# Blocks of 64 tokens of two head pairs in place of chunks of 128 tokens of one pair in a chunked RWKV-7 scan

## The chip, the cores and the metric

The kernel runs on one core of one Trainium2 chip. The metric is the device time of one execution, from the first to the last instruction on the slowest (here the only) core, in microseconds (us). It is written for the engines directly: each engine has its own list of instructions, in the order in which the program writes them, and semaphores are the only link between engines.

## What is computed

One layer of a bidirectional RWKV-7 model on 1024 latent and 128 context tokens, width 1024, 16 heads of 64. Only the scan matters here. For each head and direction it runs over the tokens:

```
def step(S, inp):
    r_t, w_t, k_t, v_t, a_t, b_t = inp
    sa = jnp.einsum('bhvk,bhk->bhv', S, a_t)
    S = S * w_t[:, :, None, :] + sa[..., None] * b_t[:, :, None, :] + v_t[..., None] * k_t[:, :, None, :]
    return S, jnp.einsum('bhvk,bhk->bhv', S, r_t)
```

The latent scans start from a given state, the context scans from zero; the context's final states are outputs. The forward and backward results are added, normalised per head (`lnx`), scaled, given a bonus term and a gate. Ahead of the scan stand the projections of all operands, behind it the output projections and the MLP.

## The kernel before, in words

Three stages follow each other. The **projection stage** goes over the 8 pairs of heads (a pair fills the 128 partitions). It projects the operands of a pair with TensorE, VectorE (DVE) makes the decays' running sums (`decay_sums`) and the operand planes (`operands`), and SyncE (SP) stores these in DRAM: `op_d`, `v_d`, and in `x_d` the inverses of the 16x16 diagonal blocks, which DVE makes by `substitution`. The **scan stage** takes them back. The **product stage** is the three 1024x1024 products and the MLP, by a seven-product scheme on quadrants.

The scan stage turns the recurrence into small matrix products over a chunk of `C = 128` tokens. Its unit is one chunk of one pair in both directions (forward chunk j and backward chunk 7-j together): `UNITS` = 8 pairs x 9 chunks = 72. The chunk's triangular system is inverted by doubling: 16 to 32 to 64 to 128 tokens, one level a round, `LATE = LEVELS - FIRST = 3` levels. Round `s` of the loop (one per engine, `for s in range(-4, UNITS)`) holds, on TensorE (PE) in this order:

- `turn(s)`: transposes of the partial inverses `xt` of the three units in flight; `token_major(s+1)`: four 128x128 transposes of the operands of the next unit; `ur_state(s)`: state times operands;
- `gram(s+4, d)` for the two directions, the products between tokens of the unit four ahead, in pieces 0, 1 (128 moving columns) and 2 (256 columns); DVE masks each into `gmat` (DVE's `gram`, L2126, 128x1024 elements);
- `serial_ur`, `serial_u`, `serial_s`, `serial_y`, `y_state`: the serial part of unit `s`. ACT copies `ur` (L1656) and `up` (L1660) out of PSUM between them; DVE's `states` makes the state of the next unit (L2180, one fused instruction per direction), which `ur_state(s+1)` waits for;
- `left(s)` and `right(s)`: one inverse level for each of the three units in flight. `left` needs `tc` (DVE `turned`, L2132), `xtb` (POOL `trimmed`) and `lm` (POOL `start_inverse`); ACT copies its result (`product_out`, L1643, tile `p`) for `right`; DVE's `summed` (L2143) adds it to `xt` for the next round. The last level's result goes through ACT (`last_blocks`) and POOL (`triangles`, L900) into `tt`, which `serial_u` reads;
- the finals of one 128-token chunk of one pair, from round 5 on: `variance`, ACT's square root (L1690), DVE's `reciprocal` (L2209), `spread` and `gate` on PE, then DVE's `scaled` (L2214, L2218, L2221), and SP stores `xa_d`. After the last unit five finals are left over (`TAIL`);
- in two rounds of each nine a piece of the modulation (`modulation`, `modulation_turned`).

In the rows of the page and the trace the PE lines are those of helpers (L972 is `mm`), so a step is told by its tiles: `inv<-ident,xt` is `turn`, `bank<-ident,ub` `token_major`, `ser<-state,ub` `ur_state`, `gbank<-ub` `gram`, `ser<-vb,gmat` `serial_ur`, `bank<-ident,fstd` `spread`, `inv<-xtb,...` `left`, `ser<-ub,state` `y_state`, `ser<-ur,tt` `serial_u`, `inv<-p,tc` `right`, `ser<-...,tok` `serial_s`, `ser<-gmat,...` `serial_y`, `bank<-gl,pl` `gate`, `bank<-bones,fsq` `variance`. Operands named `64*64` use a quarter of the array (one of two row halves and one of two column halves), `128*64` half of it. Each f32 product shows as two matmul records, a transpose as one.

## Time and profile before

| | |
|---|---|
| median of 3 runs | 2689.25 us (2687.86 to 2693.72) |
| span of the profiled execution | 2688.9 us, with 67501 instructions |
| PE busy | 2568.6 us, 96% |
| DVE busy | 1872.8 us, 70% |
| ACT busy | 1081.2 us, 40% |
| POOL busy | 1188.7 us, 44% |
| chain that ended last | PE 85%, DVE 8%, issue, ACT and DMA 2% each |

The profile gives no other time of the profiled execution than its span; the span is 0.35 us under the median of the runs. PE's busy time counts a matmul from its start to its modelled end, so neighbours overlap and a gap shorter than about 0.2 us (the length of the shortest matmul record) does not show. The difference between the starts of two steps is what a step costs. The granted clock of PE is 1.00 nearly throughout, and 0.5 where it is at half speed.

### The profile page before, as it was taken

Reading aid. Unit: us, or ns where it says so; the run is one execution under the profiler, and the core shown is the slowest. Engines: PE = TensorE matmul, PEld = TensorE weight load, DVE = VectorE, ACT = ScalarE, POOL = GpSimd, SP = SyncE. Lnnn points to the kernel's source line nnn. Section 1 sums busy time; section 2 is a strip of 40 time slices with the busy share of each in tenths; the row PEclk is TensorE's granted clock in tenths of the full one; section 3 lists DMA queues with packets and bytes.
Section 4 is the critical chain, followed back from the end, with each engine's and each line's share of the span. In section 5 each row is a group of like instructions: output and inputs, shape, how many; then the busy total and the mean of one; then the engine's idle time right before and its main releaser. Section 6 shows DMA issues by size and latency. Waiting matters only on the chain.

```text
span 2688.9 us, 67501 instructions
## 1 busy us (share of the span) xinstructions
PE 2568.6 (96%) x28608; PEld 2413.9 (90%) x28608; DVE 1872.8 (70%) x2978; ACT 1081.2 (40%) x1978; POOL 1188.7 (44%) x1154
## 2 busy tenths in 40 slices
PE   4899999999999998999999998999799999999998
PEld 3899999999999996777777777999799999999998
DVE  3365675856758565787666657799778678677686
ACT  3434243342433422433333333443453453443534
POOL 1323232322323225555555545656446556565662
PEclk8999999999999999999999998999899999999999
DMA  8333425334254364445454456453223332333231
GB/s 325 106 102 118 140 71 186 113 111 140 80 175 123 101 203 116 131 133 149 142 155 139 145 162 181 133 179 98 61 63 86 81 101 63 87 82 100 63 79 71
DMA packets 282409, 329.10 MB, mean 122 GB/s; under 512 B 76288, under 2 KB 215936, under 8 KB 273536
## 3 DMA queue, kind: packets, MB, share of 16 engines
q1 hardware_dynamic: 274448, 278.66, 33.4%
q0 software_dynamic: 5904, 39.32, 6.9%
q10 hardware_dynamic: 1760, 6.82, 0.6%
q8 instruction: 228, 3.74, 0.6%
q14 instruction: 69, 0.57, 0.1%
HBM read 221.83 MB, written 91.36 MB: 116 GB/s over the span
## 4 chain that ended last, share of the span: by engine, by line
PE 85%; DVE 8%; issue 2%; ACT 2%; DMA 2%; SPq 1%; POOL 0%; DVEq 0%; ACTq 0%; POOLq 0%
PE ser L972 18%; PE gbank L972 13%; PE inv L972 11%; PE bank L972 11%; PE gbank L1416 8%; PE inv L1416 8%; PE ser L1416 7%; PE bank L1416 7%; DVE a_sum L2323 1%; DMA ring<-in_wblocks 1%; PE inv L1174 1%; DVE a_sum L2327 1%; PE bank L1157 1%; DVE a_sum L2331 1%; DVE a_lo L2297 1%
## 5 line engine op out<-in xcount | busy, mean ns | idle before, releaser
L954 POOL TENSOR_TENSOR w_lo<-raw_w,w_hi 128x512 fp32r<-128x512 f32 x264 | 427.3, 1632 | 366.9 <-ACT w_hi L1756 366.9
L849 POOL TENSOR_TENSOR wsp<-ring,wsp 128x1024 fp32r<-128x1024 f32 x67 | 205.2, 3063 | 653.9 <-ACT wsp L1518 653.9
L1756 ACT ACTIVATE w_hi<-raw_w 128x512 fp32r<-128x512 f32 x264 | 165.2, 633 | 261.6 <-PE ser L1416 98.4
L972 PE MATMUL ser<-xn_hi,wsp 128*128 128x384 f32 x816 | 217.1, 339 | 6.0 <-POOL xn_lo L855 6.0
L1416 PE MATMUL gbank<-a_hi,w_hi 128*128 128x288 f32 x616 | 185.8, 302 | 30.8 <-POOL w_lo L954 14.6
L972 PE MATMUL gbank<-xn_hi,wsp 128*128 128x384 f32 x800 | 212.6, 339 | 0.3 <-issue 0.3
L972 PE MATMUL bank<-xn_hi,wsp 128*128 128x384 f32 x800 | 210.2, 337 | 0.5 <-issue 0.5
L972 PE MATMUL inv<-xn_hi,wsp 128*128 128x384 f32 x800 | 210.4, 338 | 0.0
L2126 DVE TENSOR_TENSOR gmat<-gbank,gmask 128x1024 f32<-128x1024 f32 x144 | 175.6, 1219 | 43.8 <-PE gbank L972 43.0
L1742 ACT ACTIVATE a_hi<-a_sum 128x1152 fp32r<-128x1152 f32 x88 | 103.0, 1172 | 224.5 <-DVE a_sum L2331 78.6
L972 PE MATMUL gbank<-ub 64*64 64x128 f32 (+1 forms) x3456 | 179.4, 310 | 9.0 <-DVE gmat L2126 7.6
L1416 PE MATMUL gbank<-a_hi,w_lo 128*128 128x288 f32 x616 | 184.6, 300 | 0.0
L1416 PE MATMUL gbank<-a_lo,w_hi 128*128 128x288 f32 x616 | 184.3, 299 | 0.0
L1416 PE MATMUL inv<-a_hi,w_lo 128*128 128x288 f32 x616 | 183.6, 298 | 0.0
L1416 PE MATMUL inv<-a_hi,w_hi 128*128 128x288 f32 x616 | 183.4, 298 | 0.0
L1416 PE MATMUL inv<-a_lo,w_hi 128*128 128x288 f32 x616 | 183.2, 297 | 0.0
L1416 PE MATMUL ser<-a_hi,w_hi 128*128 128x288 f32 x616 | 181.5, 295 | 1.5 <-ACT r L1795 1.5
L1416 PE MATMUL bank<-a_hi,w_lo 128*128 128x288 f32 x616 | 181.7, 295 | 0.0
L1416 PE MATMUL ser<-a_hi,w_lo 128*128 128x288 f32 x616 | 181.7, 295 | 0.0
L1416 PE MATMUL ser<-a_lo,w_hi 128*128 128x288 f32 x616 | 181.3, 294 | 0.0
L1416 PE MATMUL bank<-a_lo,w_hi 128*128 128x288 f32 x616 | 181.3, 294 | 0.0
L1416 PE MATMUL bank<-a_hi,w_hi 128*128 128x288 f32 x616 | 181.2, 294 | 0.0
(402 smaller groups left out, 7541.1 us busy)
## 6 DMA issues: line engine op xcount, KB each, us to landing
ring<-in_wblocks SPq DMA_DIRECT2D x107, 512.0 KB, 5.3
ub<-op_d SPq DMA_DIRECT2D x144, 256.0 KB, 2.8
raw_w<-in_wquads SPq DMA_DIRECT2D x33, 1024.0 KB, 4.8
raw_w<-in_wquads POOLq DMA_DIRECT2D x22, 1024.0 KB, 9.5
op_d<-ar SPq DMA_DIRECT2D x32, 576.0 KB, 5.4
op_d<-bk SPq DMA_DIRECT2D x32, 576.0 KB, 6.2
raw_w<-in_wquads SPq DMA_DIRECT2D x44, 256.0 KB, 3.7
raw_w<-zsum POOLq DMA_DIRECT2D x11, 1024.0 KB, 13.1
```

The source lines that it names most:

```text
L849: GT(wsp[s % 2][1][:], ring[(N_ADA_RING + s) % RING][:], wsp[s % 2][0][:].bitcast(F32), ALU.subtract).then_inc(S["wsplit_lo"], 1)
L954: GT(w_lo[n % 4][:], src, w_hi[n % 4][:].bitcast(F32), ALU.subtract).then_inc(S["wl_ok"], 1)
L972: return nc.tensor.matmul(out, lhsT, rhs, start=start, stop=stop)
L1157: ins = nc.tensor.transpose(banks[3][:, y * P:(y + 1) * P], ub[v % LOADS][:, y // 2, 2 + y % 2, :], ident[:])
L1174: ins = nc.tensor.transpose(inv[:, 0, x * P:(x + 1) * P], xt[:, place_of(v), :, :].rearrange("p h t -> p (h t)"), ident[:])
L1416: return nc.tensor.matmul(out, lhsT, rhs, start=start, stop=stop, skip_group_check=True)
L1742: A(a_hi[:, places2(q, j), :], src, ACT.Copy).then_inc(S["ah_ok"], 1)
L1756: A(w_hi[s][:], raw_of(op)[:, m, :].rearrange("p (k c) -> p k c", k=KH), ACT.Copy).then_inc(S["wh_ok"], 1)
L2126: V.tensor_tensor(gmat[v % SETS][:, d, :, :, :].rearrange("p h x t -> p h (x t)"), gbank[:, :, :], gmask[:, d:d + 1, :].to_broadcast([P, 2 ...
L2297: V.tensor_tensor(a_lo[:, places2(q, j), :], src, a_hi[:, places2(q, j), :].bitcast(F32), sub).then_inc(S["al_ok"], 1)
L2323: ch.step(V.tensor_tensor(o[j], a11[j], a12[j], sub))
L2327: ch.step(V.tensor_tensor(o[j], o[j], a22[j], add))
```

## The change

The unit becomes one block of 64 tokens of **two** pairs in both directions (a group of two pairs has `NB` = 18 blocks; 4 groups x 18 = 72 units again). Each operand of 128 columns or rows that held 128 tokens of one pair now holds 64 tokens of pair 0 and 64 of pair 1. The doubling ends at 64 tokens, so `LEVELS` goes to 5 and two levels are in flight (`LATE` = 2). `last_blocks` and its semaphore `tt_ok` are gone, and `triangles` is two full-height instructions. The operands for two units arrive together (`double_in`, 7 DMAs per two units, in place of 5 per unit). DVE's running sums are over 64 tokens, 18 in place of 9 per direction. `states` is two instructions of 128x256. `y` moves from the bank of `ser` to that of `inv`. The round's order on every engine is rewritten, and grams are made three units ahead, not four. In the last group two finals are done per round, so that two and not five are left for after the last unit.

```diff
-LEVELS = 6
+LEVELS = 5
...
-SETS = 5
...
+GROUPS = PAIRS // 2
+UNITS = GROUPS * NB
+SETS = 4
+DOUBLES = 4
...
 def finals(s):
 
...
+    g, j = divmod(s, NB)
...
-
-
-TAIL = [(PAIRS - 1, FIN_ORDER[i], NC * (PAIRS - 1) + i) for i in range(4, NC)]
+    if j >= FIN_FROM:
+        if g + 1 == GROUPS:
+            return [item(g, 2 * (j - FIN_FROM) + x) for x in range(2)]
...
-        op_d = scratch("op_d", [PAIRS, 2, NC, P, 4, C])
-        v_d = scratch("v_d", [PAIRS, NC, P, P])
+        ar_d = scratch("ar_d", [GROUPS, 2, NC, P, 2, 2, C])
+        bk_d = scratch("bk_d", [GROUPS, 2, NB, P, 2, 2, HD])
+        v_d = scratch("v_d", [GROUPS, NC, P, 2, P])
...
+            def double_in(n):
+
...
+                    sp.wait_ge(S["y_full"], 2 * (n - DOUBLES) + 2)
+                sp.dma_start(xt[:, 2 * q:2 * q + 2, :, :].rearrange("p u h t -> p (u h t)"), x_d[g, c].rearrange("p u h t -> p (u h t)")).then_inc(u_in[q], 16)
+                for d in range(2):
+                    m = chunk(d, c)
+                    sp.dma_start(ub[q][:, d, 0:4, :].rearrange("p x t -> p (x t)"), ar_d[g, d, m].rearrange("p x b t -> p (x b t)")).then_inc(u_in[q], 16)
+                    sp.dma_start(ub[q][:, d, 4:8, :].rearrange("p (u x) t -> p u (x t)", u=2), bk_d[g, d, 2 * m:2 * m + 2].rearrange("u p x b t -> p u (x b t)")).then_inc(u_in[q], 16)
+                    sp.dma_start(vb[q][:, d, :, :], v_d[g, m]).then_inc(u_in[q], 16)
...
-            for s in range(-4, UNITS):
+            for s in range(-LATE, UNITS):
+                if there(s):
...
-                    start_inverse(s + 3, 2)
-                if there(s + 1):
-                    triangles(s + 1)
...
+            def gram(v, d):
+
...
+                for h in range(2):
+                    hs = halves_of[h]
+                    for b in range(2):
+                        mm(banks[h][halves_of[b], gram_at(d, 0, 1)], moving_of(v, d, b)[hs, 0, :], still_of(v, d, 0)[hs, b, :], True, True)
+                for h in range(2):
+                    hs = halves_of[h]
+                    for b in range(2):
+                        mm(banks[h][halves_of[b], gram_at(d, 1, 2)], still_of(v, d, 0)[hs, b, :], moving_of(v, d, b)[hs, 1, :], True, True)
...
                     for h in range(2):
-                        for i in range(2):
-                            b, other = halves_of[i], halves_of[1 - i]
-                            if lev < LEVELS - 1:
-                                ins = mm(inv[halves_of[h], i, to], lm[v % 2][lev - FIRST][b, h, :], xtb[b, x, h, :], True, True)
-                            else:
-                                ins = mm(inv[halves_of[h], i, to], gmat[v % SETS][b, 1 - i, h, 0, other], xtb[b, x, h, :], True, True)
+                        for b in range(2):
+                            ins = mm(inv[halves_of[h], b, to], lm[v % 2][lev - FIRST][halves_of[b], h, :], xtb[halves_of[b], x, h, :], True, True)
                 ins.then_inc(S["p1_full"], 1)
...
             def y_state(u):
...
+                pe.wait_ge(S["xt_ok"], sums(round_of(u) + 1))
+                for d in range(2):
+                    for b in range(2):
                         for hs in halves_of:
-                            mm(ser[hs, 1, y_at(j, d)], state[d][j % 2][hs, :], ub[q][hs, d, 1, :], d == 0, False)
+                            ins = mm(inv[hs, b, y_at(j, d)], state[x][hs, b, d, :], moving_of(u, d, b)[hs, 1, :], d == 0, False)
...
                             for h in range(2):
...
-                                ins = mm(ser[hs, 0, 3 * P + d * HD:3 * P + (d + 1) * HD], tok[u % TOKS][:, h, 2 * d + x, :],
-                                         vb[q][:, d, hs] if x else up[:, h, d, :], x == 0, x == 1)
+                                for b in range(2):
+                                    bs = halves_of[b]
+                                    ins = mm(ser[hs, b, 2 * P + d * HD:2 * P + (d + 1) * HD], tok[u % TOKS][bs, h, 2 * d + x, :],
+                                             vb[q][bs, d, token_half(d, u), hs] if x else up[bs, h, d, :], x == 0, x == 1)
                     ins.then_inc(S["s_full"], 1)
...
-                j, q, g = u % NC, u % LOADS, gmat[u % SETS]
+                j, q, g = u % NB, set_of(u), gmat[u % SETS]
+                pe.wait_ge(S["ys_full"], u + 1)
...
                     for d in range(2):
-                        for h in range(2):
-                            hs = halves_of[h]
-                            first = j == NC_LAT and x == 0 and d == 0
-                            last = x == 1 and d == 1
-                            ins = mm(ser[hs, 1, y_at(j, d)], vb[q][:, d, hs] if x else up[:, h, d, :], g[:, d, h, part, :], first, last)
+                        for turned in range(2):
+                            for h in range(2):
+                                hs, b = halves_of[h], h ^ turned
+                                bs = halves_of[b]
+                                ins = mm(inv[hs, b, y_at(j, d)], vb[q][bs, d, token_half(d, u), hs] if x else up[bs, h, d, :], g[bs, d, h, part, :], False, (x, d) == (1, 1))
                 ins.then_inc(S["y_full"], 1)
 
...
-            for s in range(-4, UNITS):
-                p, j = divmod(s, NC)
-                inverses, serial, ahead = in_flight(s), there(s), there(s + 4)
-                if inverses:
-                    turn(s)
+            for s in range(-LATE - 1, UNITS):
+                m, j = divmod(s, NC)
+                inverses, serial, ahead = in_flight(s), there(s), there(s + 3)
+                if serial:
+                    serial_free(s)
+                    for x in finals(s - 1):
+                        variance(*x)
+                    ur_state(s)
                 if there(s + 1):
                     token_major(s + 1)
                 if serial:
-                    ur_state(s)
+                    serial_ur(s)
+                if inverses:
+                    turn(s)
                 if ahead:
-                    gram(s + 4, 0, (0, 1, 2))
+                    gram(s + 3, 0)
                 if serial:
-                    serial_ur(s)
-                    if j == 4:
-                        pe.wait_ge(S["ada_ok"], p + 1)
+                    serial_u(s)
                 for x in finals(s - 1):
+                    if x[1] == NC_LAT:
+                        gate(*x)
                     spread(*x)
                 if inverses:
                     left(s)
+                    right(s)
                 if serial:
+                    if j == 2:
+                        modulation(m)
+                    if j == 3:
+                        modulation_turned(m, s)
+                    serial_s(s)
                     y_state(s)
                 if ahead:
-                    gram(s + 4, 1, (0, 1))
+                    gram(s + 3, 1)
+                for x in finals(s):
+                    if finals(s)[0][2]:
+                        pe.wait_ge(S["xa_ok"], finals(s)[0][2])
+                    (mean if x[1] == NC_LAT else gate)(*x)
                 if serial:
-                    serial_u(s)
-                    if j == 2:
-                        modulation(p)
-                if inverses:
-                    right(s)
-                if ahead:
-                    gram(s + 4, 1, (2,))
-                for x in finals(s):
-                    mean(*x)
-                if serial:
-                    serial_s(s)
                     serial_y(s)
-                    if j == 3:
-                        modulation_turned(p)
-                for x in finals(s):
-                    gate(*x)
-                    variance(*x)
+            pe.wait_ge(S["gram_ok"], 2 * UNITS)
...
+                ch.step(V.tensor_tensor(dst[:], ser[:, :, 2 * P:3 * P].rearrange("p b (d v) -> p b d v", d=2), scale_of(u), mul))
+                ch.settle()
+                V.tensor_tensor(dst[:], dst[:], stg[:], add).then_inc(S["s_ok" if j < NB - 1 else "sf_ok"], 1)
...
-            for s in range(-4, UNITS):
-                p, j = divmod(s, NC)
+            for s in range(-LATE - 1, UNITS):
+                m, j = divmod(s, NC)
+                if there(s - 1):
+                    y_add(s - 1)
+                if there(s):
+                    carried(s)
+                if in_flight(s):
+                    turned(s)
+                if NC <= s < NC + SUB - 1:
+                    substitution(PAIRS - 1, [s - NC], [0])
+                if there(s + 3):
+                    gram(s + 3, 0)
                 for x in finals(s - 1):
                     reciprocal(*x)
-                if there(s) and j == 4:
-                    dve.wait_ge(S["mt_full"], p + 1)
-                    V.tensor_tensor(mods[:, 4 * p + 16:4 * p + 20, :], banks[2][:, 3 * P:3 * P + 8].rearrange("p (b c) -> p b c", c=2),
-                                    bc(vec[:, 4 * p + 16:4 * p + 20], 2), add).then_inc(S["ada_ok"], 1)
-                if there(s - 1):
-                    y_add(s - 1)
-                if in_flight(s):
-                    turned(s)
-                if there(s):
-                    carried(s)
-                if NC <= s < NC + SUB - 1:
-                    substitution(PAIRS - 1, [s - NC], [0])
-                if there(s + 4):
-                    gram(s + 4, 0)
-                for x in finals(s - 1):
-                    scaled(*x)
+                scaled(finals(s - 1))
                 if NC <= s < NC + SUB - 1:
                     substitution(PAIRS - 1, [s - NC], [1])
                 if in_flight(s):
                     summed(s)
+                if s == -1:
+                    first_state(0)
+                if there(s):
+                    if j == 3:
+                        modulated(m, s)
+                    states(s)
+                    if s % NB == NB - 1 and s + 1 < UNITS:
+                        first_state(s // NB + 1)
                 for x in finals(s):
-                    centred(*x)
-                if there(s):
-                    states(s)
-                    if j == NC_LAT and p + 1 < PAIRS:
-                        first_state(p + 1)
-                if there(s + 4):
-                    gram(s + 4, 1)
+                    if x[1] == NC_LAT:
+                        centred(*x)
+                if there(s + 3):
+                    gram(s + 3, 1)
```

PE's order in one round with a final and no modulation. Before:

```order
L1174 MATMUL inv<-ident,xt 128x128 x3
L1157 MATMUL bank<-ident,ub 128x128 x4
L972 MATMUL ser<-state,ub 64x64 x8
L972 MATMUL gbank<-ub 64x128 x8
L972 MATMUL gbank<-ub 64x256 x4
L972 MATMUL ser<-vb,gmat 64x64 x8
L972 MATMUL bank<-ident,fstd 64x128 x2
L972 MATMUL inv<-xtb,gmat 64x64 x4
L972 MATMUL inv<-xtb,lm 64x64 x8
L972 MATMUL ser<-ub,state 64x128 x4
L972 MATMUL gbank<-ub 64x128 x8
L972 MATMUL ser<-ur,tt 64x64 x8
```

Behind these stand `inv<-p,tc` x12, `gbank<-ub` 64x256 x4, four rows of `serial_s`, `serial_y` with 128 columns, `gate` and `variance`. The same engine and place in the changed kernel, from `ur_state` on:

```order
L1054 MATMUL ser<-state,ub 64x64 x8
L1246 MATMUL bank<-ident,ub 128x128 x4
L1054 MATMUL ser<-vb,gmat 64x64 x8
L1264 MATMUL inv<-ident,xt 128x128 x2
L1054 MATMUL gbank<-ub 64x64 x8
L1054 MATMUL gbank<-ub 64x128 x4
L1054 MATMUL ser<-ur,tt 64x64 x8
L1054 MATMUL bank<-ident,fstd 64x128 x2
L1054 MATMUL inv<-xtb,lm 64x64 x8
L1054 MATMUL inv<-p,tc 64x64 x8
L1054 MATMUL ser<-up,tok 64x64 x4
```

`right` (`inv<-p,tc`) now follows `left` directly, where `y_state`, a gram and `serial_u` stood between them; `spread` (`bank<-ident,fstd`) stands behind `serial_u`, and each gram has half the columns. The rest of the round is `serial_s` with 16 products in all, `y_state`, the other gram, `gate`, `serial_y` with 64 columns x16, and `variance`.

DVE's order in the same round, before (`yf` rows are `scaled`, `state` rows `states`):

```order
L2209 RECIPROCAL fstd<-fstd 128x2
L2132 TENSOR_TENSOR tc<-inv,trimc 128x384
L2165 TENSOR_SCALAR stg<-state,gstep 128x64 x2
L2126 TENSOR_TENSOR gmat<-gbank,gmask 128x1024
L2214 TENSOR_TENSOR yf<-yf,bank 128x128
```

And in the changed kernel:

```order
L2215 TENSOR_TENSOR stg<-state,gstep 128x256
L2181 TENSOR_TENSOR tc<-inv,trimc 128x256
L2175 TENSOR_TENSOR gmat<-gbank,gmask 128x512
L2251 RECIPROCAL fstd<-fstd 128x2
L2257 TENSOR_TENSOR yf<-yf,bank 128x128
L2261 SCALAR_TENSOR_TENSOR yf<-yf,pl,fbon 128x128
L2264 SCALAR_TENSOR_TENSOR yf<-yf,pl,bank 128x128
L2190 TENSOR_TENSOR xt<-inv,xt 128x256
L2226 TENSOR_TENSOR state<-ser,gstep 128x256
L2228 TENSOR_TENSOR state<-state,stg 128x256
```

The reciprocal that `spread` waits for has moved from the head of the round to behind the first mask (`gmat`), and the state is made by two instructions, one after the other.

## Rows read from the trace of the kernel before

**Rows 1.** Windows view of stages: us, busy (x count) per engine, PE clock, DMA share, GB/s.

```profile
134.00:1010.00 876.00, 874.17 (x6054) 854.33 (x6052) 571.25 (x916) 339.92 (x518) 250.62 (x79) 1.00 0.41 128
1030.00:1598.00 568.00, 561.37 (x13975) 448.00 (x13974) 388.79 (x917) 221.68 (x598) 298.72 (x650) 1.00 0.48 141
```

**Rows 2.** Timeline of PE, one round: start, us, engine, line, op, tiles, shape, count.

```profile
1282.56 0.55 PE L1174 MATMUL inv<-ident,xt 128*128 128x128 f32 x3
1282.94 0.60 PE L1157 MATMUL bank<-ident,ub 128*128 128x128 f32 x4
1283.47 0.46 PE L972 MATMUL ser<-state,ub 64*64 64x64 f32 x16
1283.76 1.05 PE L972 MATMUL gbank<-ub 64*64 64x128 f32 x24
1284.74 0.69 PE L972 MATMUL ser<-vb,gmat 128*64 128x64 f32 x16
1285.25 0.39 PE L972 MATMUL bank<-ident,fstd 128*64 128x128 f32 x4
1285.57 0.34 PE L972 MATMUL inv<-xtb,gmat 64*64 64x64 f32 x8
...
1285.97 0.49 PE L972 MATMUL ser<-ub,state 64*64 64x128 f32 x5
...
1286.96 0.69 PE L972 MATMUL ser<-ur,tt 128*64 128x64 f32 x16
1287.57 0.58 PE L972 MATMUL inv<-p,tc 64*64 64x64 f32 x24
1287.97 0.61 PE L972 MATMUL gbank<-ub 64*64 64x256 f32 x8
1288.40 0.40 PE L972 MATMUL bank<-yf,bones 64*64 64x128 f32 x4
1288.73 0.34 PE L972 MATMUL ser<-up,tok 128*64 128x64 f32 x4
...
1289.25 0.61 PE L972 MATMUL ser<-gmat,up 128*64 128x128 f32 x8
...
1290.12 0.39 PE L972 MATMUL bank<-gl,pl 128*64 128x128 f32 x4
...
1290.51 0.55 PE L1174 MATMUL inv<-ident,xt 128*128 128x128 f32 x3
```

**Rows 3.** Timeline of PE, the first `turn` of unit 0 and of unit 71.

```profile
1029.57 0.52 PE L1174 MATMUL inv<-ident,xt 128*128 128x128 f32 x3 [0.75 <-DVE xt L2143]
...
1597.59 0.33 PE L1174 MATMUL inv<-ident,xt 128*128 128x128 f32 x1
```

**Rows 4.** Groups by line and form, 1075 to 1546 us: xcount, busy us, mean ns, idle before.

```profile
L2126 DVE TENSOR_TENSOR gmat<-gbank,gmask 128x1024 f32<-128x1024 f32 x116 | 141.4, 1219 | 26.7 <-PE gbank L972 26.1
L2218 DVE SCALAR_TENSOR_TENSOR yf<-yf,pl,fbon 128x128 f32<-128x128 f32 x57 | 25.5, 447 | 2.9 <-DVE yf L2214 0.9
L2143 DVE TENSOR_TENSOR xt<-inv,xt 128x256 f32<-128x256 f32 x50 | 21.2, 424 | 56.7 <-PE inv L972 56.7
```

**Rows 5.** Timeline, all engines: `left` on 16 records and the ACT copy behind it.

```profile
1020.17 0.46 PE L972 MATMUL inv<-xtb,lm 64*64 64x64 f32 x16 [0.42 <-issue]
1020.69 0.38 ACT L1643 ACTIVATE p<-inv 128x256 f32<-128x256 f32 x1 [4.91 <-PE inv L972]
```

**Rows 6.** Windows view around the falls of the clock (columns as in rows 1).

```profile
1011.00:1020.00 9.00, 5.54 (x115) 3.30 (x115) 4.68 (x7) 0.28 (x1) 3.64 (x8) 1.00 0.25 40
1020.00:1023.00 3.00, 2.37 (x56) 1.94 (x56) 1.32 (x2) 0.38 (x1) 0.46 (x2) 0.67 0.25 23
1602.00:1605.00 3.00, 2.89 (x38) 2.29 (x36) 0.54 (x2) 1.18 (x4) 0.00 (x0) 0.50 0.72 273
```

**Rows 7.** Groups by line and form, DVE, 140 to 1008 us.

```profile
L1988 DVE TENSOR_TENSOR_SCAN ar<-ones,ar 128x128 f32<-128x128 f32 x126 | 41.3, 402 | 125.2 <-ACT ar L1587 125.2
L2072 DVE TENSOR_SCALAR kk<-kk 128x1152 f32<-128x1152 f32 x8 | 6.1, 760 | 71.5 <-ACT kk L1538 71.5
```

643 lines of the change are left out of this document (316 added, 327 removed).

## The prediction

> **What bounds the kernel now.** I read the stages first, then one round on PE, then who waits for whom. In the windows of stages [rows 1] PE is busy for 874 of 876 us in the projection stage and 561 of 568 us in the scan stage, at full clock; DVE is busy for about two thirds of each, and DMA moves 141 GB/s in the scan. So PE sets the time of both. The first `turn` of unit 0 and of unit 71 stand at 1029.57 and 1597.59 us [rows 3], 568.0 us for 71 units, 8.0 us each. In one round on PE [rows 2] the steps follow each other without a visible wait; the start of a step less the start of the one before is its cost. The reader is to see that nothing on PE waits there: the other engines' work fits beside it. The change halves PE's columns, so the question is whether PE will still be fed.
>
> **PE's work per unit.** Between the two `turn` rows lie 7.95 us, of which the mean (`yf,bones`) is 0.33 and comes once a pair, so 7.62 [rows 2]. By parts:
>
> - `gram`, both directions: 16 records of 128 columns and 8 of 256 cost 0.98 us, which is 31 ns per 128 columns on a quarter tile. 64-column records on quarter tiles cost 0.40/24 = 17 ns each (`left`, from 1285.57 to 1285.97, and `right`, 1287.57 to 1287.97). The new gram has 16 records of 64 and 8 of 128: 0.27 + 0.25 = 0.52. Two of them: 1.04 for 1.96, -0.92.
> - `turn`, three transposes in 0.38, becomes two: -0.13. `left` and `right`, 24 records in 0.40 each, become 16: -0.26 together.
> - `serial_y`, 16 records of 128 columns on half tiles in 0.87, becomes 32 of 64 columns on quarter tiles at 17 ns: 0.54, -0.33.
> - `serial_s`, 16 records on half tiles in 0.52, becomes 32 on quarter tiles, 0.54: +0.02.
> - `serial_ur` (0.51) and `serial_u` (0.61) keep 16 records of 64 columns. Their new tiles are quarters, but only the two on the diagonal are used, so two run side by side as before: 0. `y_state` has twice the records at half the columns, again on the diagonal: +0.05, between 0 and +0.1.
>
> Sum -1.57, which leaves 6.05 us.
>
> **Changes of tile shape.** `spread` is 4 records of 128 columns and costs 0.32, where `serial_y` needs 0.87/16 = 0.054 each, 0.22 for four: 0.10 more, and behind it the tile shape changes from half to quarter. By the shapes in the same rows a round now has 7 changes: whole array (`turn`, `token_major`), quarter (`ur_state`, gram), half (`serial_ur`, `spread`), quarter (`left` to gram), half (`serial_u`), quarter (`right`, gram), half (`serial_s` to `variance`), whole. The new round has 10: quarter (`ur_state`), whole (`token_major`), quarter (`serial_ur`), whole (`turn`), quarter (gram, `serial_u`), half (`spread`), quarter (`left` to gram), half (`gate`), quarter (`serial_y`), half (`variance`), quarter. Three more at 0.10 are +0.30: 6.35 us. The Trainium skill, TensorEngine Tiling (Array Packing), Key Properties, states that changing the tiling mode drains TensorE; it speaks against this order of steps. By that rule the three changes stay in the sum, and the cost behind `spread` agrees; without it the forecast would be 0.3 us a unit, some 20 us, lower.
>
> **New waits.** Here the order decides. Prices of the handovers: after the last record of `left` was issued (about 1020.44, 0.27 after its start) the ACT copy of 128x256 began at 1020.69 and took 0.38 [rows 5], so 0.25 us pass from PE to ACT; back to PE I take 0.06, between nothing and the 0.25 of the other way.
> - (a) `right` follows `left` at once, and needs ACT's copy of it: 0.25 + 0.38 + 0.06 = 0.69 us idle on PE in every round. In the kernel before, `y_state`, a gram and `serial_u` (1.6 us, rows 2) covered this.
> - (b) `spread` waits for the reciprocal, which on DVE now stands behind the mask of the first gram. The mask takes 1.22 us for 1024 elements and the add 0.42 for 256 [rows 4], so 1.04 ns an element and 0.15 fixed; 512 elements take 0.69 and the reciprocal of 2 the fixed 0.15. From the gram's end: 0.15 to DVE + 0.69 + 0.15 + 0.06 = 1.05, against 0.6 for `serial_u`: 0.45 idle.
> - (c) `y_state` waits for `summed`, behind `right` and `scaled` on DVE: its three instructions of 128 elements take 0.45 by the row of the middle one [rows 4] and 0.28 for each other by elements, 1.0 together. With 0.25 from PE and the add's 0.42 that way and the way over `left`, `right` and `serial_s` meet within 0.1: 0.12 idle. `serial_u` waits for `ur` and for the square root behind it on ACT: 0.1.
> - The state takes 2 x 0.42 in place of 2 x 0.22 (64 elements each), but gram, `gate` and `serial_y` (1.4 us) lie over it before the next `ur_state`: 0 where a unit has one final. If that cover were gone it would cost 0.4 us a unit.
>
> Waits sum to 1.36, less 0.15 because a drain and a wait at the same place overlap: 6.35 + 1.2 = **7.55 us** for a unit with one final, against 7.75 to 7.95 now. Bounds: 7.15 (64-column records at the 15.5 ns of their columns, and (b) half hidden) and 8.05 (each wait 0.1 longer, since what waits can't load its weights early).
>
> A unit without a final loses (b), (c), `spread`, `gate` and `variance`: about 6.2 (5.95 to 6.6). A unit of the last group with two finals puts a second `scaled` (1.0 us) ahead of `summed` on DVE, and so ahead of `y_state` and of the state: 9.3 (9.0 to 9.8).
>
> **The sum.** Units 0 to 10 have no final (11 x 6.2 = 68), units 11 to 64 one (54 x 7.55 = 408), 65 to 70 two (6 x 9.3 = 56); today's 568 us, less 5 units without a final at 7.0, 63 at 7.8 and three without grams at 6, leave 24 us for modulations and means, which stay (23); the last two of these units lack a gram (-2). Scan: 553 for 568, **-15**.
>
> Start: before unit 0 four rounds run, now three, and with half the mask: -4 (0 to -6). End: three finals fewer behind the last unit, about 1 us of DVE each, but two in the last unit: -3 (0 to -5), with PE at half clock there as now [rows 6].
>
> **What costs nothing.** In the projection stage 18 scans of 64 in place of 9 of 128 per direction: 402 ns by the mean for 128 [rows 7], of which I take 0.15 as fixed: a pair of short scans costs 0.15 more, 2.7 us a pair of heads, between 0 and 7 if a short scan cost as much as a long one. DVE then sits idle 71.5/8 = 8.9 us a pair before `kk` [rows 7], and PE never waits. If that cover were gone it would be 8 x 2.7 = 22 us. The stores of `bk` go in runs of 64 elements: more packets, on a queue with 8 pairs' time for it. `double_in` issues 7 DMAs in two rounds instead of 10, three rounds ahead of use. POOL loses half of its `tt` work. The masks shrink by 0.53 us each; DVE was not the bound.
>
> Total: -15 - 4 - 3 = -22 from the profiled 2688.9, so 2667 us; the runs' median is 0.35 above that span, which changes nothing.
>
> **Rivals.**
> 1. *The columns count in full.* PE hides the waits, since part of what I call a wait is the drain that I count too: 7.15, 5.95 and 9.0 a unit. Scan 66 + 386 + 54 + 21 = 527, with start and end -8: -50, 2639 us. For it: now nothing waits and 1.57 us go. Against it: (a) has no work at all in between.
> 2. *The handovers eat it (slower).* Each of the waits costs more: 8.05, 6.6 and 9.8. Scan 73 + 435 + 59 + 21 = 588, +20, with start and end -7: +13, 2702 us. The place is `left`/`right` and `spread` on PE; it decides from 7.9 us a one-final unit on. For it: three engines now take turns within the round, and (b) hangs on DVE's queue. Against it: each handover in the trace is short.
> 3. *No change to be measured*: 7.75 to 7.9 a unit, 2684 to 2694 us.
> 4. *The clock falls.* Between 1011 and 1020 us PE was busy 5.54 of 9 us by its records at full clock; in the next 3 us the granted clock was 0.67, part of them at the lower level of 1.2 GHz, and at 1602 to 1605 it was 0.50, all of it [rows 6]. At that level the round's 6.35 us of PE work double and the waits vanish: some 12 us. In a fifth of the rounds that is 14 x 4.5 = +63, 2730 us. Against it: the new round has about 1.2 us of waits in 7.55, some 85% busy and no gap over 0.7. The Trainium skill, TensorE: Matmul & The Clock Gate, "A second HAM failure mode: psum-queue depth-cycling", tells of a kernel whose clock swings because PE idles shortly between groups; the trace shows a fall only behind a stretch that was 62% busy.
>
> That the change doesn't do what it says is no rival: order and shapes are plain.
>
> **How the numbers follow.** A measurement tells from no change about 0.2%, 5.4 us. Forecast (-22, with its own bounds 2650 to 2683) 0.42; rival 1 0.19; rival 3 0.15; rival 2 0.18; rival 4 0.06. Faster 0.61, same 0.15, slower 0.24. The range takes in rivals 1 and 2 and leaves out the clock: 2638 to 2708.
>
> **What would show it.** On PE's timeline after: `turn` of two records in 0.26; each gram 0.52; an idle of 0.5 to 0.7 before `inv<-p,tc` released by ACT's `p`, and one of 0.3 to 0.5 before `spread` released by DVE's `fstd`; units of 7.5 us in the middle, 6.2 at the start, 9.3 in the last group; clock 1.00 from 1030 on. The projection stage unchanged within 2 us. The forecast is wrong if units of the middle take under 7.2 or over 7.9 us, or if the clock is under 0.95 in the scan.

## The result and the profile of the changed kernel

The changed kernel takes 2745.54 us (median of 4 runs, 2736.75 to 2749.04), the kernel before 2688.91 beside it: a ratio of 1.0207, interval 1.0186 to 1.0227. It is 57 us slower where I forecast 22 us faster, outside my range. Times and ratios are medians; every row of a trace comes from one execution, here of 2749.04 us, so it can differ from the median by some us.

The page of the changed kernel: busy time, then the slices.

```profile
span 2747.1 us, 70639 instructions
PE 2536.8 (92%) x30456; PEld 2383.7 (87%) x30456; DVE 1834.6 (67%) x3070; ACT 1015.0 (37%) x1829; POOL 1109.7 (40%) x925
...
PE   4999999999999998888888887999889999999998
```

PE is busy for 92% and not 96%, all of it lost in the slices of the scan. The two stages in the windows view, columns as in [rows 1]:

```profile
134.00:1010.00 876.00, 870.58 (x6018) 850.73 (x6017) 577.15 (x1038) 339.56 (x517) 262.51 (x78) 1.00 0.43 128
1022.00:1671.00 649.00, 547.95 (x16005) 433.30 (x16007) 350.28 (x880) 159.65 (x463) 210.23 (x432) 0.95 0.42 128
```

From the first `ur_state` to that of unit 71 now lie 647.5 us (1022.58 to 1670.05); in the kernel before, 568.1 (1030.46 to 1598.55). That is +79. The first `ur_state` is 8 us earlier, the way from the last one to the first product 13 us shorter (19.5 for 32.1), the products take the same (1057.6 for 1058.3): together +58, the difference of the spans. So the scan holds the whole loss. Who PE waited for in it (us in total, times, longest):

```profile
PE inv L1054 <- ACT p L1713: 35.7, 71, 0.5
PE bank L1054 <- DVE fstd L2251: 19.9, 44, 0.6
PE ser L1054 <- issue: 12.4, 11, 3.1
PE inv L1054 <- issue: 11.8, 7, 2.9
PE inv L1054 <- DVE xt L2190: 5.8, 13, 1.2
PE bank L1246 <- issue: 3.9, 1, 3.9
...
```

Two things are in it. The rows with a releaser are waits between steps, 61.4 us here and 67.5 with three small rows that I left out; I had forecast the first two and sized them well. The rows that end in "issue" are times in which PE waited for nothing that the profile's semaphores show, 30.5 us in all; before there were 1.7. Here is one undisturbed round, and the disturbed one ahead of it:

```profile
1557.60 0.45 PE L1054 MATMUL gbank<-ub 64*64 64x64 f32 x15
1559.78 0.49 PE L1054 MATMUL gbank<-ub 64*64 64x64 f32 x9 [1.72 <-issue]
1560.05 0.96 PE L1054 MATMUL ser<-ur,tt 64*64 64x64 f32 x16
...
1567.74 0.46 PE L1054 MATMUL ser<-state,ub 64*64 64x64 f32 x16
1568.13 0.66 PE L1246 MATMUL bank<-ident,ub 128*128 128x128 f32 x4
1568.72 0.68 PE L1054 MATMUL ser<-vb,gmat 64*64 64x64 f32 x16
1569.33 0.44 PE L1264 MATMUL inv<-ident,xt 128*128 128x128 f32 x2
1569.70 0.68 PE L1054 MATMUL gbank<-ub 64*64 64x64 f32 x24
1570.20 0.64 PE L1054 MATMUL ser<-ur,tt 64*64 64x64 f32 x16
1571.27 0.44 PE L1054 MATMUL bank<-ident,fstd 128*64 128x128 f32 x4 [0.42 <-DVE fstd L2251]
1571.64 0.46 PE L1054 MATMUL inv<-xtb,lm 64*64 64x64 f32 x16
1572.60 0.46 PE L1054 MATMUL inv<-p,tc 64*64 64x64 f32 x16 [0.50 <-ACT p L1713]
1572.88 0.30 PE L1054 MATMUL ser<-up,tok 64*64 64x64 f32 x8
...
1573.61 0.62 PE L1054 MATMUL inv<-ub,state 64*64 64x64 f32 x13
...
1574.68 0.44 PE L1054 MATMUL bank<-gl,pl 128*64 128x128 f32 x4
1575.05 0.46 PE L1054 MATMUL inv<-gmat,up 64*64 64x64 f32 x16
```

The undisturbed round takes 8.14 us (the next `ur_state` is at 1575.88). In the first rows a gram of 24 records stops after 15 of them and goes on 1.7 us later. No semaphore stands between these products; the stretch is inside a step. There are 15 such stretches of over 0.6 us, and behind some of them the granted clock is at its lower level:

```profile
1083.00:1089.00 6.00, 5.50 (x110) 4.53 (x112) 1.17 (x3) 1.64 (x4) 0.00 (x0) 0.50 0.02 7
1294.00:1297.00 3.00, 3.00 (x73) 2.98 (x76) 1.01 (x4) 0.00 (x0) 1.44 (x3) 0.51 1.07 361
```

The first comes at the end of a stretch of 3.92 us, which ends at 1082.65. The second comes without one. These are the rows ahead of it:

```profile
1291.74 0.44 PE L1054 MATMUL bank<-ident,fstd 128*64 128x128 f32 x4 [0.42 <-DVE fstd L2251]
1293.08 0.46 PE L1054 MATMUL inv<-p,tc 64*64 64x64 f32 x16 [0.50 <-ACT p L1713]
1293.47 1.37 PE L1054 MATMUL ser<-sel,mrow 128*128 128x2 f32 x8
```

Behind the two waits stand eight records of `modulation_turned` (four products), which have two columns each and take over 1 us. The clock fell twelve times inside the scan. Six falls follow a stretch. Three (at 1294, 1379 and 1543) follow the two waits and the eight records of two columns; one (1321) follows the two waits and a third of 0.64 before `y_state`. The other two stand near the scan's ends, behind waits of 1.44 and 1.20. No fall of this trace follows the two short waits alone, which stand in most rounds. The clock of 0.95 over 649 us is 32 us of lost time.

PE's instructions come by DMA as well; the list of queues shows them as q8. Over the scan, before and then after:

```profile
q8 instruction: 111, 1.82, 1.3%
```

```profile
q8 instruction: 128, 2.10, 1.4%
```

Packets of 16 KB (1.82 MB / 111). At 128 for 16005 matmul records with as many weight loads, one packet is 250 instructions, so about 125 records with their loads. My theory A: a packet waits behind the data that `double_in` now brings at once for two units (1.4 MB). The rival B: PE's rows of 64-column records (17 ns each) use instructions faster than packets can come. Rival C: the clock falls because of the waits between steps.

### The profile page after: what moved, and what is told of

Its sections match the earlier page's. It is cut to its first block, busy times and chain, and to the rows that moved or that the text cites. A ratio compares the mean times of both kernels' runs of the same rounds, so it can differ in the third digit from the quotient of the medians.

```text
span 2747.1 us, 70639 instructions
## 1 busy us (share of the span) xinstructions
PE 2536.8 (92%) x30456; PEld 2383.7 (87%) x30456; DVE 1834.6 (67%) x3070; ACT 1015.0 (37%) x1829; POOL 1109.7 (40%) x925
## 4 chain that ended last, share of the span: by engine, by line
PE 48%; DVE 10%; issue 3%; ACT 2%; POOL 0%; DMA 0%; DVEq 0%; ACTq 0%; POOLq 0%
PE gbank L1486 8%; PE inv L1486 8%; PE ser L1486 7%; PE bank L1486 7%; PE inv L1054 5%; PE ser L1054 5%; PE gbank L1054 3%; PE bank L1054 3%; PE bank L1246 2%; DVE a_sum L2362 1%; DVE gmat L2175 1%; PE inv L1264 1%; DVE a_sum L2366 1%; DVE a_sum L2370 1%; ACT p L1713 1%
## 5 line engine op out<-in xcount | busy, mean ns | idle before, releaser
L936 POOL TENSOR_TENSOR wsp<-ring,wsp 128x1024 fp32r<-128x1024 f32 x67 | 216.5, 3232 | 645.6 <-ACT wsp L1588 645.6
L985 POOL TENSOR_TENSOR tt<-xt,ttm 128x128 f32<-128x128 f32 x144 | 62.0, 452 | 373.2 <-DVE xt L2190 373.2
L1054 PEld LDWEIGHTS ser<-xn_hi,wsp 128*128 128x128 f32 x816 | 148.9, 188 | 8.5 <-POOL xn_lo L942 6.7
```

The lines of the kernel that those rows point to most:

```text
L936: GT(wsp[s % 2][1][:], ring[(N_ADA_RING + s) % RING][:], wsp[s % 2][0][:].bitcast(F32), ALU.subtract).then_inc(S["wsplit_lo"], 1)
L985: GT(tt[v % 2][:, d, :, :], xt[:, place_of(v), :, :], two(ttm[:, d, :]), ALU.mult).then_inc(S["tri_ok"], 1)
L1054: return nc.tensor.matmul(out, lhsT, rhs, start=start, stop=stop)
```

## The experiments

Each ratio is to the kernel before run beside it, whose median lay between 2688.6 and 2694.2 us. For each run the table gives the scan (first to last `ur_state`), the sum of PE's "issue" rows in it, the sum of its other rows, the clock's loss (one less the granted clock, times the length; the clock is given to 0.01, so within some 3 us), and what is left of the scan: PE's work. The column "profiled" is the time of the execution that the trace shows; all columns behind it belong to that one, and it lies up to 11 us from the median.

| kernel | us | ratio | profiled | scan | issue | waits | clock | work |
|---|---|---|---|---|---|---|---|---|
| before | 2689 | 1 | 2689 | 568 | 2 | 4 | 0 | 562 |
| e2_bundled | 2694 | 1.001 | 2696 | 566 | 0 | 4 | 0 | 563 |
| changed | 2746 | 1.021 | 2749 | 648 | 31 | 68 | 32 | 517 |
| e1_split | 2732 | 1.015 | 2729 | 620 | 14 | 70 | 19 | 517 |
| e7_light | 2727 | 1.013 | 2721 | 616 | 13 | 70 | 12 | 521 |
| e8_gate | 2741 | 1.018 | 2745 | 637 | 31 | 72 | 32 | 502 |
| e3_spread | 2704 | 1.005 | 2715 | 600 | 15 | 58 | 24 | 503 |
| e4_both | 2701 | 1.003 | 2711 | 597 | 14 | 61 | 18 | 504 |
| e5_order | 2720 | 1.010 | 2723 | 611 | 24 | 58 | 31 | 498 |
| e6_quarters | 2716 | 1.010 | 2717 | 604 | 29 | 50 | 24 | 501 |
| e10_twice | 2755 | 1.024 | 2760 | 642 | 19 | 4 | 7 | 613 |
| e11_order2 | 2691 | 1.001 | 2691 | 581 | 38 | 19 | 23 | 501 |
| e12_light2 | 2683 | 0.996 | 2683 | 569 | 31 | 20 | 23 | 495 |
| e13_even | 2699 | 1.002 | 2696 | 580 | 22 | 21 | 17 | 520 |
| e14_even4 | 2707 | 1.005 | 2702 | 589 | 31 | 21 | 18 | 519 |
| e15_even2 | 2686 | 0.998 | 2680 | 567 | 28 | 12 | 6 | 521 |

### Loads in halves, and the kernel before with bundled loads

```diff
-                if s % 2 and s // 2 + DOUBLES < UNITS // 2:
-                    double_in(s // 2 + DOUBLES)
+                n, h = divmod(s - 1, 2)
+                if s and n + DOUBLES < UNITS // 2:
+                    double_in(n + DOUBLES, (h,))
```

> The changed kernel, but the seven loads for two units are issued in two halves, one unit apart. Theory A (instruction supply): PE's long idle stretches inside a step (13 of over 0.6 us that nothing releases, 27 us in all) come from its 16 KB instruction packets, which queue behind 1.4 MB of data issued at once; the clock falls behind them. Then at most 3 such stretches stay, the clock in the scan rises from some 0.945 to 0.98 or more, and the time is 2747 - 27 - 25 = about 2695 us. Rival B (PE's dense rows of short products outrun the instruction supply whatever the data traffic): the stretches stay, 2740 to 2750. Rival C (the clock falls because of the waits between the steps, not because of these stretches): stretches gone, clock as now, about 2720.

The other way round, in the kernel before:

```diff
-                if s + LOADS < UNITS:
-                    unit_half(s + LOADS, 0)
-                    unit_half(s + LOADS, 1)
+                if s % 2 and s - 1 + LOADS < UNITS:
+                    sp.wait_ge(S["y_full"], s + 1)
+                    for v in range(s - 1 + LOADS, min(s + 1 + LOADS, UNITS)):
+                        unit_half(v, 0)
+                        unit_half(v, 1)
```

> The kernel before, with the loads of two units issued together every second round instead of one unit's in each. Theory A: the kernel before then shows the idle stretches too, 4 or more of over 0.6 us (now 1 in the scan), and is slower by 8 to 50 us: 2697 to 2740. Rival B: its PE order has not changed, so 2686 to 2693 and at most 2 stretches.

e1: 2731.9 us (ratio 1.0148, 1.0132 to 1.0163); the "issue" rows fall from 31 to 14 us, the clock's loss from 32 to 19. A gain of 14, where A wanted 52. e2: 2694.0 (1.0008, 0.9998 to 1.0019), with 0.4 us of "issue": the kernel before takes the same bundles of 1.4 MB without any stretch. Theory A alone has fallen: bundles of this size do nothing to the kernel before. What A needs and e2 lacks is in PE's own order; the halves take 17 us of "issue" out of the changed kernel, so bundling has a share there.

### The handovers

```diff
+                if inverses:
+                    left(s)
                 for x in finals(s - 1):
...
                     spread(*x)
                 if inverses:
-                    left(s)
                     right(s)
```

> The changed kernel with spread moved from before left to between left and right. Theory W (the two handovers are plain latencies that other work can cover): the waits before spread (0.42) and before right (0.50) shrink to about 0.17 and 0.15, a unit with one final takes 7.5 to 7.6 us instead of 8.14, 59 units of these give -35 us: about 2712, with the long stretches as they are. Rival: the later spread makes DVE's three scaled instructions and so summed late, y_state waits in its place, units stay at 8.0 or more and the time over 2738.

> Both edits. If they are independent: 2747 - 52 - 35 = about 2660 us, under the kernel before by 1%. If the clock falls because of the waits between steps (rival C), fewer waits alone bring it up: e3 then gains more than 35. If rival B holds: about 2710.

e3: 2704.2 (1.0050, 1.0031 to 1.0069); e4: 2701.4 (1.0034, 1.0020 to 1.0048). One line moved gives 41 us, but not as I had written: an undisturbed unit takes 7.73 and not 7.55. The rival was right on the place. In e4 `y_state` waits for `xt`, behind DVE's `scaled`:

```profile
1335.53 0.62 PE L1056 MATMUL inv<-ub,state 64*64 64x64 f32 x13 [0.64 <-DVE xt L2193]
```

So half of the two covered waits went on to the next step. The rest of the gain is stretches (31 to 15), clock (32 to 24) and the work column (517 to 503), which also holds the short gaps that the modelled ends of the products hide. The halves add 3 us here at most: the two intervals overlap.

### Less traffic, and the shape change

e7 is the changed kernel with smaller loads of `ub` and `vb` (most units compute with operands of an earlier one, so part of the work's input is left out, but no instruction):

```diff
+                r = slice(0, P if n < DOUBLES else 16)
...
-                    sp.dma_start(vb[q][:, d, :, :], v_d[g, m]).then_inc(u_in[q], 16)
+                    sp.dma_start(vb[q][r, d, :, :], v_d[g, m, r]).then_inc(u_in[q], 16)
```

> The changed kernel, where from the fifth pair of units on the loads of operands and values (ub, vb) bring 16 of 128 partitions, so most of each unit's operands are those of an earlier unit (work left out; the instructions of every engine stay). Traffic falls from 1.4 MB per two units to 0.28. Theory A (PE's instruction packets wait behind the data): the idle stretches inside steps (15, 28 us, in the changed kernel; 10, 13 us, with the loads in halves) fall to 2 or fewer, nearly all half-clock stretches inside the scan go too (48 us of them before, worth 24), time 2747 - 28 - 22 = 2690 to 2700. Rival B (PE's dense rows alone outrun the supply): 8 or more stretches stay, over 2715. Rival C (waits between steps bring the clock down): stretches gone, half-clock time in the scan still over 30 us, 2715 to 2725.

e7: 2727.4 (1.0131, 1.0111 to 1.0151). The traffic of the scan falls from 128 to 74 GB/s, the "issue" rows from 31 to 13 us, but 8 stretches of over 0.6 us stay. So these loads have a share; it does not follow that traffic has no more, since the other transfers (`ring` in pieces of 512 KB, `fbon`, `xt`, `xa_d`) go on. Four of its falls of the clock again come behind the two waits and the eight records of two columns. In e3, where in seven of the eight rounds with these records the wait before `right` is gone and the other is at most 0.33 us, none of the eight has a fall, nor has the kernel before, without either wait. So rival C holds for a part: short waits count where such records stand behind them.

e8 moves `gate` next to `variance`:

```diff
-                for x in finals(s):
...
                 if serial:
                     serial_y(s)
+                for x in finals(s):
...
+                    (mean if x[1] == NC_LAT else gate)(*x)
```

> The changed kernel with gate moved behind serial_y, next to the following variance, which has its tile shape: two changes of tile shape fewer in a round with a final. At the 0.10 us of the prediction a unit takes 7.95 instead of 8.14, at the 0.15 to 0.18 that the trace after suggests 7.8, and 54 to 59 units give -11 to -19 us: 2727 to 2736. If a change of tile shape costs nothing by itself: 2745, unit 8.14. The state of the next unit has the same time as before, so no new wait is expected.

e8: 2740.7 (1.0180, 1.0157 to 1.0202). Undisturbed units take 7.8 us for 8.14, `gate` 0.27 for 0.37: the change of shape costs what the second line of the expectation said. The total shows 5 of the 18 us, and its interval overlaps that of the changed kernel: the expected 2727 to 2736 was missed. The work column falls by 15, the profiled start was 5 us later, and more of the units were disturbed.

### Taking the waits away

e5 adds to e4 (DVE first, then PE; `gate` also goes behind `serial_y`):

```diff
-                scaled(finals(s - 1))
...
                     states(s)
...
+                scaled(finals(s - 1))
...
                     serial_s(s)
-                    y_state(s)
                 if ahead:
                     gram(s + 3, 1)
+                if serial:
+                    y_state(s)
```

> Loads in halves and spread between left and right, as in e4, and in addition: DVE does summed and the state ahead of scaled, PE does the second gram ahead of y_state, and gate behind serial_y. In e4 a unit with one final takes 7.73, of which PE waits 0.64 for xt before y_state. Theory W: summed can start 0.25 after right, so y_state waits for nothing; with two changes of tile shape less a unit takes 6.9 to 7.1, and the time is 2701 - 59 x 0.7 = about 2660, under the kernel before by 1%. Rival: the supply of instructions cannot follow (the stretches inside steps rise from 10 to 20 or more) and the time stays over 2685.

e6 issues each half of the loads in two parts, half a round apart:

```diff
+                if s and ahead + DOUBLES < UNITS // 2:
+                    sp.wait_ge(S["u_ok"], s + 1)
+                    double_in(ahead + DOUBLES, (h,), (1,))
```

> e5 with the loads of two units in four parts, two in each round, one at the round's start and one behind its middle, 0.4 MB each. Theory A: the idle stretches inside steps fall to 3 or fewer, and the time is another 10 to 25 us under e5. If they depend on PE's own density alone, the same as e5.

e5: 2719.6 (1.0098, 1.0082 to 1.0115), 18 us slower than e4. Waits for `xt` are gone, but the late `scaled` made a new one, and the stretches came back:

```profile
PE bank L1056 <- DVE yf L2268: 32.6, 44, 2.0
PE inv L1056 <- issue: 14.6, 13, 2.0
```

The first is `gate`, which waits for the final before. I had not priced what was queued behind the step that I moved. e6: 2716.3 (1.0095, 1.0080 to 1.0110), with more "issue" (29 for 24): shorter bursts don't help here, and the 3 us between the two medians are within their intervals.

### The supply of instructions by itself

The first of the rows added in e9, in the kernel before, ahead of its first round:

```diff
+            for i in range(256):
+                for h, b in quarter:
+                    M(banks[h][halves_of[b], 0:HD], ident[halves_of[h], halves_of[b]], ident[halves_of[h], 0:HD], start=True, stop=True)
```

> The kernel before, with rows of products on constants put in between the projection and the scan, read on PE's timeline by line. (1) 1024 products of 64 columns on quarter tiles, 2048 records, 4096 instructions with their weight loads, in a row without any wait. Theory B (the supply of instructions has a ceiling; 256 of them, one 16 KB packet, arrive no more often than each 3.3 to 3.5 us, the shortest distances seen in all traces so far): the row takes 16 x 3.4 = 54 us, 27 ns a record, with pauses. If there is no such ceiling, 2048 x 17 ns = 35 us. (2) 256 products of 128 columns on quarter tiles: 512 x 31 ns = 16 us either way. (3) 128 on half tiles; (4) the products of (2) and (3) mixed with 128 changes of shape; (5) 64 on the whole array; (6) those of (2) and (5) mixed with 128 changes. A change of shape costs ((4) - (2) - (3)) / 128: 0.10 us by the prediction, 0.15 to 0.18 by the steps of the changed kernel; (6) likewise for quarter and whole.

PE's timeline of the first row, 2048 records without a wait:

```profile
1054.18 2.09 PE L1359 MATMUL gbank<-ident 64*64 64x64 f32 x128 [1.64 <-issue]
1057.94 2.09 PE L1359 MATMUL gbank<-ident 64*64 64x64 f32 x128 [1.67 <-issue]
1061.41 2.10 PE L1359 MATMUL gbank<-ident 64*64 64x64 f32 x128 [1.38 <-issue]
1064.88 2.10 PE L1359 MATMUL gbank<-ident 64*64 64x64 f32 x128 [1.38 <-issue]
...
1069.14 14.73 PE L1362 MATMUL gbank<-ones 64*64 64x128 f32 x509
1083.80 14.19 PE L1365 MATMUL gbank<-bones 128*64 128x128 f32 x256
```

This is rival B, plain: 128 records in 2.09 us, then a pause, again and again, with a new start every 3.47 us (1057.94, 1061.41, 1064.88). 128 records with 128 weight loads are 256 instructions, one 16 KB packet if an instruction has 64 bytes (16 KB / 256). The row takes 58.9 us (1010.11 to 1069.04) where 2048 records at 2.09/128 need 33. It is one execution, and for two stretches of 6.8 us in it (from 1019.8 and from 1043.7) the clock was at its lower level; of the rows shown only that of 1042.40, below, reaches into one. The Trainium skill, Runtime: NRT & Kernel Launch, "Instruction fetch mechanics", describes such a stream in blocks of 16 KiB, 256 instructions, and calls the cost of crossing from one block to the next mostly hidden; the block agrees with x128, "hidden" does not hold in this row. The records of 128 columns behind it run without a pause, 28.6 ns each (14.66 us for 512): 3.66 us for a packet's worth, just over 3.47. The same row earlier, and windows of it with clock, DMA's share and GB/s at the end:

```profile
1033.56 2.10 PE L1359 MATMUL gbank<-ident 64*64 64x64 f32 x128 [1.91 <-issue]
1037.57 2.09 PE L1359 MATMUL gbank<-ident 64*64 64x64 f32 x128 [1.91 <-issue]
1042.40 2.66 PE L1359 MATMUL gbank<-ident 64*64 64x64 f32 x128 [2.74 <-issue]
```

```profile
1030.00:1034.00 4.00, 2.09 (x144) 1.95 (x136) 0.00 (x0) 0.00 (x0) 0.00 (x0) 1.00 0.48 145
1038.00:1042.00 4.00, 1.67 (x115) 1.53 (x106) 0.00 (x0) 0.00 (x0) 0.00 (x0) 1.00 0.60 180
1058.00:1062.00 4.00, 2.62 (x168) 2.48 (x171) 0.00 (x0) 0.00 (x0) 0.00 (x0) 1.00 0.01 4
```

With 100 to 145 GB/s of data a new 128 begins every 4.0 us, at 180 GB/s once after 4.83; with DMA idle every 3.47, at 1054 still 3.76. Single distances are no clean measure (one of 4.0 lies at 28 GB/s, from 1014.88), but the longest one stands under the most data.

The trace also has start and length of each instruction packet. In the quiet part a packet starts 1.12 us after PE has gone on, takes 0.94 and PE goes on again 1.41 after it has landed: together 3.47. The same holds for the changed kernel, and answers what PE waited for there. In each of its 15 stretches PE goes on 1.2 to 1.5 us after a packet has landed, and each of these packets is late: between its start and that of the one before lie 164 to 259 matmul records (once 103), where 125 is the mean. What stood ahead of it were data:

```profile
1078.26:1080.26 2.00, 0.47 (x34) 0.47 (x23) 0.88 (x2) 0.38 (x1) 1.67 (x4) 1.00 0.96 353
1555.37:1557.37 2.00, 2.00 (x51) 1.62 (x42) 0.21 (x1) 0.40 (x2) 1.34 (x3) 1.00 0.92 339
1557.37:1559.78 2.41, 0.69 (x18) 0.38 (x18) 0.42 (x1) 1.01 (x3) 0.00 (x0) 1.00 0.07 19
```

The first two windows are the 2 us before the packets of the stretches that end at 1082.65 and 1559.78, at 353 and 339 GB/s; the third shows the queues nearly idle once that packet had started. I counted this for all packets of the scan, those with over 200 GB/s of data in the 2 us before their start and the others, and how many of each are followed by a stretch of over 0.6 us:

| kernel | packets behind data | with a stretch | other packets | with a stretch |
|---|---|---|---|---|
| before | 62 | 1 | 49 | 0 |
| e2_bundled | 59 | 0 | 52 | 0 |
| changed | 49 | 15 | 78 | 0 |
| e7_light | 25 | 8 | 102 | 0 |
| e10_twice | 62 | 10 | 75 | 2 |
| e11_order2 | 63 | 21 | 64 | 1 |
| e12_light2 | 30 | 21 | 96 | 0 |

So in these kernels A and B are two halves of one cause. Of the 26 packets of the changed kernel with 160 records or more between their start and the one before, 22 stand behind data; but in the kernel before, and in e2 with the same bundles, such bursts leave PE enough instructions, and with PE's dense rows they don't. How a burst holds a packet back inside the queues no run shows.

The shape changes: row (4) of the expectation took 47.89 us, so (47.89 - 14.66 - 14.13)/128 = 0.149 us a change between quarter and half; row (6) took 51.04, so (51.04 - 14.66 - 14.49)/128 = 0.171 between quarter and whole.

PE's dense rows put into the kernel before: `for v, lev in in_flight(s) * 2` in `left` and `right`.

> The kernel before with every product of left and of right issued twice (same results): 48 records more per unit, in two rows of 48 at 17 ns. No ceiling in supply: +0.8 us a unit, 71 x 0.8 = +57 us, 2749, at most 2 idle stretches inside steps. Theory B: those rows run the supply dry, 8 or more stretches of over 0.6 us appear in a kernel whose data traffic is unchanged, and the time is 2765 or more.

```profile
PE inv L972 <- issue: 11.2, 8, 2.1
PE ser L972 <- issue: 7.3, 10, 1.9
```

e10: 2754.5 (1.0244, 1.0227 to 1.0261). A kernel that had 2 us of "issue" now has 19, 12 stretches of over 0.6 us in the scan, with its traffic unchanged. The total of +66 is less than the 76 that I wanted at least, so B's time was missed (the doubled rows themselves cost 51 us of work, not 57); the count of stretches is B's.

### Can the change pay?

e11 is e5 with `gate` in the next round, between `left` and `spread`:

```diff
                 for x in finals(s - 1):
-                    if x[1] == NC_LAT:
-                        gate(*x)
+                    if finals(s - 1)[0][2]:
+                        pe.wait_ge(S["xa_ok"], finals(s - 1)[0][2])
+                    gate(*x)
+                for x in finals(s - 1):
                     spread(*x)
```

> e5 with gate moved to the next round, between left and spread (PE waited 0.66 us, 39 times, for DVE's last scaled instruction before gate in e5). Gate and spread have one shape and stand together, and both cover ACT's copy for right. Without the supply's ceiling: 2719.5 - 26 (that wait) - 59 x 0.2 (two changes of shape less) = about 2682, under the kernel before by 0.4%. Theory B: fewer waits leave the supply less time to catch up, the stretches inside steps grow from 20 us to 30 or more, and the time is 2690 to 2705.

```profile
PE inv L1056 <- issue: 22.5, 19, 3.2
```

e11: 2691.1 (1.0005, 0.9993 to 1.0017), as fast as the kernel before. The waits are down to 19 us, an undisturbed unit takes 6.64, and "issue" is up to 38 us: what the waits gave up the supply took in part. 6.64 is near the supply's own floor: 226 records a unit (16005/71 by the windows row) at 3.47/128 are 6.1 us, at 4.0/128 they are 7.1.

e12 is e11 with the loads of e7, so it too leaves out part of the input. e13 moves `token_major`, on ACT too, and in the eight rounds that have it also the first piece of the modulation, to behind `serial_y` (not shown); e14 is e13 with the four parts of e6:

```diff
                     ur_state(s)
-                if there(s + 1):
-                    token_major(s + 1)
...
                     serial_s(s)
+                if there(s + 1):
+                    token_major(s + 1)
                 if ahead:
```

> e11 with the operand and value loads cut to 16 of 128 partitions from the fifth pair of units on (most operands are those of an earlier unit; work left out, instructions kept). Data traffic lengthens the distance of packets (3.47 us in the quiet part of e9's row, 4.0 where DMA moved 100 to 180 GB/s). If that is what makes the stretches, they fall from 34 us to under 15 and the time to under 2675; if PE's demand alone is over the quiet supply, over 20 us stay and the time is over 2680.

> e11 with token_major (four transposes in 0.6 us, the step with the fewest instructions per time) moved from behind ur_state to between serial_s and the second gram, in the middle of the round's densest row (right to the next ur_state, 140 records in about 3.0 us, where one packet of 128 records with their weight loads takes at least 3.47 us), and modulation behind serial_y. Same instructions, same traffic, same number of shape changes. Theory B: the stretches inside steps fall from 23 (34 us) to 12 or fewer (under 20 us), with fewer half-clock stretches behind them, and the time falls by 10 to 25 us, to 2665 to 2682, under the kernel before. If only traffic and the mean rate of instructions count: no change, 2686 to 2696.

> e13 with the loads in four parts as in e6. If the residual stretches depend on the length of data bursts: another 5 to 10 us less. As e6 gained only 3 us over e5, I expect 0 to -5 against e13.

e12: 2683.1 (0.9964, 0.9952 to 0.9975). With these loads nearly gone 31 of 38 us of "issue" stay, which by my expectation says that PE's demand alone is over the supply. The table of packets says less: 79 of 141 GB/s of traffic stay, and all of its 21 stretches follow a packet behind 231 to 389 GB/s of the other transfers. What e12 shows is that in this dense order most packets behind a burst (21 of 30) empty PE, where it was 1 of 62 in the kernel before. e13: 2699.0 (1.0023, 1.0008 to 1.0038). Same instructions, two steps moved: "issue" falls from 38 to 22 us and the clock's loss from 23 to 17, as B wants, but the time does not fall to the 2665 to 2682 that I expected, since the work grew by 19. By the traces `serial_ur` right behind `ur_state`, on the same sums in PSUM, starts 0.55 us after it (0.39 for the next step before), and seven of the eight rounds with that piece take 10.3 to 12.0 us, where e11 needs 8.6 to 9.9. e14: 2706.7 (1.0051, 1.0033 to 1.0068): four parts make it worse, a miss.

e15, in the rounds with j == 2:

```diff
+                early = serial and j == 2
+                if there(s + 1) and early:
+                    token_major(s + 1)
```

> e13 with the old places of token_major and modulation in the eight rounds that hold a modulation. If its cost there was the place of modulation (rounds of 10.4 for 8.8 us), 8 x 1.6 = 13 us come back and the gain of the even supply stays: 2699 - 13 = 2686, between 2680 and 2690, under the kernel before by 0.1 to 0.4%. If the stretches inside steps come back in these rounds or elsewhere, 2695 or more.

e15: 2686.3 (0.9977, 0.9967 to 0.9988): 60 us under the changed kernel and 0.2% under the kernel before. The rounds with the modulation gave back 12.0 us of the 13 expected. That the rest came out is partly luck: "issue" rose again from 22 to 28 us, and the falls in waits (21 to 12) and clock (17 to 6) had not been forecast. The unit's size is then worth something, but little.

## Why the prediction was wrong, point by point

- **What bounds the kernel**: right for the kernel before. The question that I put, whether PE will still be fed, was the right one; I looked for the answer at engines and semaphores only, and not at the queue that brings PE its own instructions.
- **The step that failed** is "What costs nothing". It costed `double_in` and the short products at nothing beyond their time. Nowhere did it count PE's instructions. The new round asks for 226 records a unit (197 before, 13989/71) in rows of 17 ns, and its densest row, from `right` at 1572.60 to the end of the next `ur_state` at 1576.28, asks for 144 records in 3.7 us, 128 in 3.3, where the supply gives 128 in 3.5 to 4.0, and a packet behind a burst of data comes later still. Missing from the sum: 29 us of stretches, and the clock's falls behind six of them.
- **The clock** (rival 4, 0.06): "a fifth of the rounds" would have been 14; there were 12 falls in 71 rounds, and 32 us instead of 63 (by the times at the lower level 34: 17 behind stretches, 7 in the four falls without one, 10 at the scan's two ends). The argument against it, "no gap over 0.7", failed through the stretches of up to 3.9 us; four falls came without one, behind two waits of 0.92 together and either eight records of two columns or a third wait, of 0.64. I had left the modulation's records out of that argument. The Trainium skill, TensorE: Matmul & The Clock Gate, "A second HAM failure mode: psum-queue depth-cycling", which I had cited, tells of a clock that swings in a kernel where PE idles briefly between groups; these four falls agree with it.
- **The unit**: 8.14 for 7.55. `turn` 0.37 (0.26 forecast, and a shape change); gram 0.50 (0.52); (a) `left` to `right` 0.96 (0.27 + 0.69 = 0.96, exact); (b) `serial_u` to `spread` 1.07 (0.61 + 0.45, exact). Too small: a shape change is 0.15 and not 0.10 (three: +0.15); (c) 0.26 before `y_state` for 0.12 (+0.14); the 0.15 taken off for overlap was not there (+0.15); the last 0.15, by difference, lies in the steps of 64-column records (`serial_y` 0.62 for 0.54, `ur_state` 0.39 for 0.29) with shape changes around them. Over 54 units that is 32 us. Rival 2 (8.05, +13 us) had this part right, and both of my signs of being wrong came: a unit of over 7.9, and a clock just under 0.95 in the scan (34 us lost in 647.5).
- **Rival 1** (columns in full) fell: PE's work went from 562 to 517 us, 45, where 1.57 less 0.30 a unit make 90.
- **The other unit kinds**: without a final 6.41 to 6.5 undisturbed (6.2 forecast, 5.95 to 6.6), with two finals 9.3 to 9.6 (9.3): right.
- **The sum**: 553 forecast + 32 (unit) + 29 (stretches) + 32 (clock) = 646, for 647.5 measured. Each of the last two terms is good to some us only, so that it closes this well is partly luck.
- **Start and end**: -4 forecast, -8 in this profile, but over all the later runs with the same start the first `ur_state` lies between 1024.5 and 1031.2, so -8 was partly luck; end -3 forecast, -13 measured. Of that some 8 us are the clock: I had left it "as now", but over the 32.1 us of the kernel before the granted clock was 0.65, over the 19.5 of the changed one 0.84 (11 us lost for 3). I did not take the rest apart.
- **Projection**: the short scans cost nothing, as forecast.

```profile
L2036 DVE TENSOR_TENSOR_SCAN ar<-ones,ar 128x64 f32<-128x64 f32 x252 | 47.4, 268 | 125.2 <-ACT ar L1657 125.2
L2121 DVE TENSOR_SCALAR kk<-kk 128x1152 f32<-128x1152 f32 x8 | 6.1, 761 | 65.1 <-ACT kk L1608 65.1
```

A scan of 64 costs 268 ns (276 by my working), so the scans take 17 us more in all (252 x 0.268 - 126 x 0.402); the idle before `kk` is still 65.1 us [rows 7], and the stage ends no later. The mask is 689 ns, as worked out (0.69):

```profile
L2175 DVE TENSOR_TENSOR gmat<-gbank,gmask 128x512 f32<-128x512 f32 x103 | 71.0, 689 | 21.9 <-PE gbank L1054 19.8
L2228 DVE TENSOR_TENSOR state<-state,stg 128x256 f32<-128x256 f32 x46 | 25.5, 553 | 1.6
```

The state's second instruction took 0.55 and not 0.42; its cover held.

**What stays open.** How a burst of data holds back an instruction packet, and how much of the stretches less traffic could take away: with smaller loads they fell from 31 to 13 us in the changed kernel, but only from 38 to 31 in e11, and spreading the same loads helped once (e1) and did nothing or harm three times (e4, e6, e14). No run took all the bursts out. Each "issue" sum is from one profile, and how far it moves between executions was not measured. And why two short waits with the eight records of two columns bring the clock down in three rounds of the changed kernel and not in the other rounds with the same rows is not settled.

## What to carry to other kernels

Count PE's instructions, not only its columns: here 128 matmul records (64 f32 products) with their weight loads came no faster than every 3.5 us in a long row, and later behind a burst of data, so long rows of records under some 27 ns each (3.47/128) run dry unless slow steps stand between them, and waits that are taken away elsewhere come back in part as a lack of instructions. Halving a tile makes more and shorter instructions; look at rows of the timeline where 128 records lie in less than 3.5 us, and at what data move just ahead of them, before calling columns saved. And when a step is moved, price what is queued behind it on every engine: one line moved in PE's order was worth 41 us, and the same care left out in e5 cost 18.

## What the runs showed of the hardware that I had not expected

- An instruction supply with a ceiling: 3.47 us per 16 KB packet with idle queues, 4.0 at 100 to 145 GB/s of data (e9); a 64-column record on a quarter tile then costs 28.8 ns in a long row (58.9 us / 2048) instead of 16.3 (2.09/128), about the 28.6 of one with twice the columns.
- Instruction packets come late behind data: all 15 stretches of the changed kernel follow one of the 49 packets with over 200 GB/s in the 2 us before, none the other 78, and PE goes on 1.2 to 1.5 us after the packet has landed.
- A change of tile shape costs 0.149 us between quarter and half and 0.171 between quarter and whole (e9).
- The granted clock can fall without a long idle stretch: at 1294 behind waits of 0.42 and 0.50 us and eight records of two columns in 1.37.
